# RWKV block inverse: 32x32 array tiles up to blocks of 32, key products inside the levels

## The reference

```python
def step(state, inp):
    r_t, w_t, k_t, v_t, a_t, b_t = inp
    sa = jnp.einsum('bhvk,bhk->bhv', state, a_t)
    state = state * w_t[:, :, None, :] + sa[..., None] * b_t[:, :, None, :] + v_t[..., None] * k_t[:, :, None, :]
    y = jnp.einsum('bhvk,bhk->bhv', state, r_t)
    return state, y
```

## Time and profile before

| | us |
|---|---|
| median of three runs | 1380.3 (lowest 1379.02, one at 3487.18) |
| the profiled execution | 1379.52 |
| its span | 1377.5 |
| TensorE busy in it | 1328.0 (96%) |
| VectorE busy | 869.5 (63%) |
| ScalarE busy | 354.0 (26%) |
| GpSimd busy | 119.6 (9%) |

### The profile page before, as it was taken

One profiled execution on the slowest core, in us unless ns is written; L12 is line 12 of the kernel. 1 busy time (PEld: TensorE's weight loads), 2 busy tenths in 40 slices (PEclk: granted clock), 3 DMA queues, 4 the chain that ended last, 5 costly groups with the idle time before them and its releaser, 6 DMA issues. The chain is left out here.

```text
span 1377.5 us, 24975 instructions
## 1 busy us (share of the span) xinstructions
PE 1328.0 (96%) x10772; PEld 1012.3 (73%) x10772; DVE 869.5 (63%) x1455; ACT 354.0 (26%) x755; POOL 119.6 (9%) x184
## 2 busy tenths in 40 slices
PE   7999999999999998899999999998999999999999
PEld 6868548689995444469998467847778765999943
DVE  4577612567778347538898567458444364798973
ACT  2311200312221014412332013703432331233300
POOL 5745000000000001010000000031000000000000
PEclk9999999999999999999999999999999999999999
DMA  8433224335444724045444543400011042454452
GB/s 303 173 129 134 104 91 153 130 138 184 175 145 171 249 73 166 0 153 184 175 145 171 206 160 123 184 1 3 4 33 34 27 160 91 154 183 147 161 183 92
DMA packets 16733, 182.30 MB, mean 132 GB/s; under 512 B 1648, under 2 KB 3952, under 8 KB 6000
## 3 DMA queue, kind: packets, MB, share of 16 engines
q1 hardware_dynamic: 14320, 175.12, 35.0%
q10 hardware_dynamic: 2304, 5.59, 1.1%
HBM read 179.65 MB, written 1.05 MB: 131 GB/s over the span
## 5 line engine op out<-in xcount | busy, mean ns | idle before, releaser
L1697 PE MATMUL banks<-xn,arena 128*128 128x128 f32 x1440 | 165.7, 275 | 0.0
L1697 PEld LDWEIGHTS banks<-xn,arena 128*128 128x128 f32 x1440 | 163.2, 192 | 0.0
L1714 PE MATMUL banks<-arena 128*128 128x512 f32 x264 | 122.0, 592 | 0.0
L1697 PE MATMUL banks<-hT,weight_ring 128*128 128x128 f32 x960 | 116.5, 275 | 0.0
L1697 PEld LDWEIGHTS banks<-hT,weight_ring 128*128 128x128 f32 x960 | 111.8, 192 | 0.0
L1423 PE MATMUL banks<-weight_ring,arena 128*128 128x512 f32 x224 | 98.7, 597 | 0.8 <-ACT arena L1313 0.8
L1714 PEld LDWEIGHTS banks<-arena 128*128 128x128 f32 x264 | 49.8, 190 | 60.7 <-issue 60.7
L1714 PE MATMUL banks<-weight_ring,arena 128*128 128x512 f32 x198 | 93.3, 592 | 0.0
L2642 DVE SCALAR_TENSOR_TENSOR arena<-arena,prm 128x255 f32<-128x255 f32 x200 | 87.4, 479 | 5.4 <-ACT arena L1068 3.6
L1423 PEld LDWEIGHTS banks<-weight_ring,arena 128*128 128x128 f32 x224 | 42.8, 193 | 51.9 <-issue 50.3
L3060 DVE COPY_PREDICATED weight_ring<-masks,banks 128x512 f32<-128x512 uint8 x48 | 35.1, 734 | 66.7 <-PE banks L2004 60.2
(11 more groups left out here) (443 smaller groups left out, 2204.7 us busy)
## 6 DMA issues: line engine op xcount, KB each, us to landing
weight_ring<-in_wall SPq DMA_DIRECT2D x81, 2048.0 KB, 8.2
weight_ring<-in_wall SPq DMA_DIRECT2D x2, 1024.0 KB, 7.2
x<-in_x_tok ACTq DMA_DIRECT2D x2, 512.0 KB, 4.6
arena<-in_mem_tok SPq DMA_DIRECT2D x1, 1024.0 KB, 17.4
arena<-in_wall SPq DMA_DIRECT2D x1, 1024.0 KB, 5.0
arena<-in_wide SPq DMA_DIRECT2D x2, 512.0 KB, 4.5
out_y<-x ACTq DMA_DIRECT2D x4, 256.0 KB, 2.0
arena<-in_masks ACTq DMA_DIRECT2D x1, 896.0 KB, 9.4
```

The lines of the kernel that those rows point to most:

```text
L1697: ins = mm(b_(n)[:, j * P:(j + 1) * P], lhsT=weights[:, kb, j * P:(j + 1) * P], rhs=features_[:, kb, :], start=opens and j == 0 and kb == ...
L1714: ins = mm(b_(n), lhsT=a, rhs=b, start=pair == 0, stop=pair == FB // 2 - 1)
```

## The change

Levels 1 to 4 and level 0 now work on blocks of 32: four 32x32 tiles on the diagonal of the array, one per 32 tokens, for eight heads per half. The inverse is kept both plain and turned (`T32`, index a), so a level needs no transposes: it has one product yl and two closing products tl. Masks repeat every 32 tokens. All four row tiles of a group write one PSUM bank (`narrow_`). The last level (32-blocks into 64) is made apart: `across_products` (group `yl..5`), `turned_diagonal` (`tf`), `turned_corners` (`to`), which ScalarE puts together in `inverse_out`. The inverse's buffer alternates between two steps, and GpSimd fills it earlier.

The order moves too: key products stand inside the levels, between yl and tl, and between the pieces of the last level; two or four `src` 1 products of a step come in the next step or at the step's end; the gates and `y_tokens(1)` come behind the last step's inverse. VectorE takes a level's copies ahead of the key product made inside that level. The order of the groups in `core_groups` is that of the TensorE code below; its removed lines are in the listing above.

```diff
-LEVELS = 6
+LEVELS = 5
...
+def core_groups(j):
+    last = j + 1 == len(STEPS)
+    later = (j, 1) if last else (j + 1, 0)
...
+    out += level_groups("yl", j, 1) + (key_products(j - 1, 1, 3) if j else key_products(0, 1, 0)) + level_groups("tl", j, 1)
...
+    out += level_groups("yl", j, 4) + key_products(*later, 0) + level_groups("tl", j, 4) + key_products(*later, 1)
...
-            b = 1 << v
-            off = (s // (2 * b) == l // (2 * b)) & (s // b != l // b) & later(s, l)
-            masks[:HD, d, 512 + HD * v:][:, :HD] = off[:HD, :HD]
-            masks[HD:, d, 512 + HD * v:][:, :HD] = off[HD:, HD:]
+            b, s_, l_ = 1 << v, s[:32], l[:, :32]
+            off = (s_ // (2 * b) == l_ // (2 * b)) & (s_ // b != l_ // b) & later(s_, l_)
+            masks[:, d, 512 + HD * v:][:, :HD] = np.tile(np.concatenate([off, off.T], axis=1), (4, 1))
...
+        def narrow_(n):
+            return bank[BANK_OF[n]].rearrange("p (a k c) -> p a k c", a=2, c=32)
+        def corners_(n):
+            return pair_(n)[:, :, 0:128].rearrange("p b (k c) -> p b k c", c=32)
...
-        T_rows = [half_of(lent[:, 2, 0, 0:1024], h) for h in HALVES]
-        Tc = [ap.rearrange("p (k b c) -> p b k c", k=4, b=2) for ap in T_rows]
-        Tt, Yb = [[quads(half_of(ap, h)) for h in HALVES] for ap in (lent[:, 2, 0, 1024:2048], lent[:, 2, 1, 0:1024])]
+        T32 = [lent[:, 2, 0, 1024 * i:1024 * i + 1024].rearrange("p (a k c) -> p a k c", a=2, c=32) for i in range(2)]
+        Yb = lent[:, 2, 1, 0:512].rearrange("p (k c) -> p k c", c=32)
...
+            def first_out(j, lv):
+                for h in HALVES:
+                    n = G[f"yl{j}{lv}{h}"]
+                    act.wait_ge(psum_full, n + 1)
+                    A(Yb[:, 8 * h:8 * h + 8, :], narrow_(n)[:, 0], ACT.Copy).then_inc(bank_sem(n), 1)
+            def inverse_out(j):
+                d = STEPS[j][0]
+                for h in HALVES:
+                    evict_pair(Tf[h], G[f"tf{j}{h}"])
+                for h in HALVES:
+                    n = G[f"to{j}{h}"]
+                    act.wait_ge(psum_full, n + 1)
+                    act.wait_ge(*when_read(G[f"tf{j}{h}"]))
+                    for r in (d, 2 + d):
+                        ins = A(Tf[h][QUARTER[r], :, :, QUARTER[1 - d]], corners_(n)[QUARTER[r]], ACT.Copy)
+                    ins.then_inc(bank_sem(n), 1)
...
+            def time_of(k, r):
+                at = (32 * r + (HD if k >= 4 else 0)) % P
+                return slice(at, at + 32)
+            def level_zero(j):
                 for h in HALVES:
...
+                    n, L = G[f"tl{j}0{h}"], heads(LA[STEPS[j][0]][h])
+                    free(n)
+                    for pp in range(2):
+                        pe.wait_ge(*when_read(G[f"ab{j}0{h}{pp}"]))
+                    for k in range(8):
+                        for a in range(2):
+                            for r in range(4):
+                                at = QUARTER[r]
+                                sides = (L[at, k, 0, time_of(k, r)], ident[at, at])
+                                ins = mm(narrow_(n)[at, a, k], lhsT=sides[a], rhs=sides[1 - a], start=True, stop=True,
+                                         tile_position=(32 * r, 32 * r))
+                    ins.then_inc(psum_full, 1)
+            def first_products(j, lv):
+                for h in HALVES:
+                    n, L, T_ = G[f"yl{j}{lv}{h}"], heads(LA[STEPS[j][0]][h]), T32[j % 2]
                     free(n)
                     pe.wait_ge(*when_read(G[f"tl{j}{lv - 1}{h}"]))
...
+                    for k in range(8):
+                        for r in range(4):
+                            at = QUARTER[r]
+                            ins = mm(narrow_(n)[at, 0, k], lhsT=L[at, k, 0, time_of(k, r)], rhs=T_[at, 0, 8 * h + k],
+                                     start=True, stop=True, tile_position=(32 * r, 32 * r))
+                    ins.then_inc(psum_full, 1)
+            def closing_products(j, lv):
                 for h in HALVES:
...
+                    n, T_ = G[f"tl{j}{lv}{h}"], T32[j % 2]
                     free(n)
                     pe.wait_ge(*when_read(G[f"yl{j}{lv}{h}"]))
...
+                    for k in range(8):
+                        for a in range(2):
+                            for r in range(4):
+                                at = QUARTER[r]
+                                sides = (T_[at, 1, 8 * h + k], Yb[at, 8 * h + k])
+                                ins = mm(narrow_(n)[at, a, k], lhsT=sides[a], rhs=sides[1 - a], start=True, stop=True,
+                                         tile_position=(32 * r, 32 * r))
+                    ins.then_inc(psum_full, 1)
+            def across_products(j):
+                d = STEPS[j][0]
+                for h in HALVES:
+                    n, L, T_ = G[f"yl{j}5{h}"], heads(LA[d][h]), T32[j % 2]
+                    free(n)
+                    pe.wait_ge(*when_read(G[f"tl{j}4{h}"]))
+                    for k in range(8):
+                        for side in range(2):
+                            first, second = 2 * side + d, 2 * side + 1 - d
+                            ins = mm(narrow_(n)[QUARTER[second], 0, k], lhsT=L[QUARTER[first], k, 0, time_of(k, second)],
+                                     rhs=T_[QUARTER[first], 0, 8 * h + k], start=True, stop=True,
+                                     tile_position=(32 * first, 32 * second))
+                    ins.then_inc(psum_full, 1)
+            def turned_diagonal(j):
+                for h in HALVES:
+                    n, T_ = G[f"tf{j}{h}"], T32[j % 2]
+                    free(n)
+                    pe.wait_ge(*when_read(G[f"tl{j}4{h}"]))
+                    for k in range(4):
+                        for swap in range(2):
+                            for r in range(4):
+                                to = r ^ (2 * swap)
+                                ins = mm(quads_(n)[QUARTER[to], swap, k], lhsT=T_[QUARTER[r], 0, 8 * h + 4 * swap + k],
+                                         rhs=ident[QUARTER[r], SIDE[r // 2]], start=True, stop=True,
+                                         tile_position=(32 * r, 32 * to))
+                    ins.then_inc(psum_full, 1)
+            def turned_corners(j):
+                d = STEPS[j][0]
+                for h in HALVES:
+                    n, T_ = G[f"to{j}{h}"], T32[j % 2]
+                    free(n)
+                    pe.wait_ge(*when_read(G[f"yl{j}5{h}"]))
+                    for k in range(4):
+                        for swap in range(2):
+                            for side in range(2):
+                                second, to = 2 * side + 1 - d, (2 * side + d) ^ (2 * swap)
+                                head = 8 * h + 4 * swap + k
+                                ins = mm(corners_(n)[QUARTER[to], swap, k], lhsT=Yb[QUARTER[second], head],
+                                         rhs=T_[QUARTER[second], 1, head], start=True, stop=True,
+                                         tile_position=(32 * second, 32 * to))
+                    ins.then_inc(psum_full, 1)
...
+            for i in range(4):
+                products(0, 0, i)
             for j in range(len(STEPS)):
...
+                later = (j + 1, 0) if j + 1 < len(STEPS) else (j, 1)
+                level_zero(j)
+                if j:
+                    products(j - 1, 1, 2)
+                if j == 2:
+                    tokens_of_keys(1, 0)
+                    tokens_of_keys(1, 1)
+                first_products(j, 1)
+                if j:
+                    products(j - 1, 1, 3)
+                else:
+                    products(0, 1, 0)
+                closing_products(j, 1)
+                for h in HALVES if j else ():
+                    x_start(j - 1, h)
+                first_products(j, 2)
+                for h in HALVES if j else ():
+                    block_solve(j - 1, h, "u1")
+                if j == 0:
+                    products(0, 1, 1)
+                closing_products(j, 2)
+                for h in HALVES if j else ():
+                    x_finish(j - 1, h)
+                if j == 0:
+                    pe.wait_ge(*when_read(G["bonus"]))
+                    transposes(G["tx_bonus"], [bonus_rows[:, tt * P:(tt + 1) * P] for tt in range(TT)])
+                first_products(j, 3)
+                for h in HALVES if j else ():
+                    block_solve(j - 1, h, "u2")
+                closing_products(j, 3)
+                for h in HALVES if j else ():
+                    y_out(j - 1, h)
+                first_products(j, 4)
+                products(*later, 0)
+                closing_products(j, 4)
+                products(*later, 1)
+                across_products(j)
+                products(*later, 2)
+                turned_diagonal(j)
+                products(*later, 3)
+                turned_corners(j)
+                if j == 0:
+                    tokens_of_keys(0, 0)
```

(69 more changed lines are left out.)

238 lines of the change are left out of this document (65 added, 173 removed).

## The result

The changed kernel takes **1521.45 us** (median of four runs, 1517.93 to 1523.48) against 1379.66 before: ratio 1.1031, interval 1.1001 to 1.1061, +142 us. The prediction said 1385, within 1362 to 1434.

The account below looks back on a forecast made before the run. TensorE, busy 1328.0 of 1377.5 us, was taken to bound the kernel. Work -12.7, waits that go -6.5 and waits that come +23.7 gave +4.5 us, so 1385 us on the median, range 1362 to 1434.

Parts of the forecast that it names:

- Price of a round: In the 32x32 inverse, one product on each tile side by side: 33 ns, bounds 27 and 60.
- rival A: In level 0, first and closing products, the round does not shrink from 60 ns: 1429 us, chance 13%.
- C: Rival: in the inverse, four row tiles writing one bank take turns, +177 us, 1562 us; chance 3%.
- Work, -12.7 us: TensorE's work on the inverse ahead of the turn of y: 88.7 us before, 76.0 after.
- Waits that go and come: TensorE's waits for VectorE's key product copies in the RWKV core: -6.5 us go, +23.7 us come.
- step 0: First step of the RWKV core: claimed to grow from 37.5 us to 42.
- Clock 1.00: In the RWKV core stage, TensorE's granted clock was claimed to stay at 1.00.
- rival E: TensorE's clock falls; at half, the inverse alone costs 76 us more, 1461 us; chance 2%.
- The arrival of instructions: Supply of TensorE's instructions in the RWKV core stage: hidden, 84 us if blocks come back to back.
- The sum of +4.5 us: Whole kernel: net of work saved, waits that go and waits that come, giving 1385 us on the median.
- rival B: Instructions arrive too slowly in the stage: 74 blocks at 3.1 us, 229 us for 191, 1423 us; chance 4%.
- The turn of y moves the end: Behind the inverse, y tile 1's turn at 1110.47 us feeds a long VectorE chain, so moving it moves the end.

Follow-up runs that it names:

- e12: Changed kernel, four heads' columns per stationary block in level 0, first and closing products (inverse not computed), VectorE taking key product first: 1383.85 us, 1.0041 of before.
- e7: Kernel before's 64x64 inverse in the change's order of work, but VectorE taking the key product ahead of the level's copies: 1378.78 us, 1.0005 of before.
- e1: Kernel before's 64x64 inverse in the change's order of work on all engines, VectorE copying the level first: 1402.14 us, 1.018 of before.
- e3: Changed kernel plus a filler product of 128x512 ahead of each of 72 groups of the inverse: 1524.73 us, 1.1066 of before.
- e4: Kernel before plus 1,024 one-column products (4,096 instructions) behind TensorE's last work: 1432.09 us, one run.
- e6: Changed kernel with VectorE taking the key product ahead of the level's two copies: 1507.23 us, 1.0935 of before.
- e9: Kernel before with the turn of y tile 1 moved ahead of the second gate: 1375.63 us, 0.9977 of before.
- e10: e7 with the turn of y tile 1 moved ahead of both gates: 1373.53 us, 0.9967 of before.

## Why the prediction was wrong, point by point

**Price of a round: right.** Before the supply runs short, level 0 of step 0 has 108 pairs in 0.91 us of TensorE's time:

```profile
928.50:929.50 1.00, 0.91 (x108) 0.94 (x110) 1.00 (x1) 0.00 (x0) 1.00 (x2) 1.00 0.00 0
```

8.4 ns a pair, 34 for a round of four against my 33. The first product's group is busy 0.74 (I had 0.72). That ends rival A. It ends C too: four row tiles write one bank here and do not take turns. The Trainium skill (TensorEngine Tiling (Array Packing), Restrictions and Gotchas) says that different row tiles cannot access one bank at the same time; taken as a price it would be four times this, and the measurement decides.

**Work, -12.7 us: not contradicted, and out of reach.** e12, which has the tiles and columns of the change and few instructions, is 8.2 us ahead of e7 at the gates, after 7.6 us of "issue" waits of its own and at a clock of 0.97. That fits the term in sign and size and does not measure it.

**Waits that go and come: right.** I had 23.7 + 1.2 = 24.9 us of waits for key products; e1 has 24.3. The net of the order was +17.2. In e1 the turn of y tile 1 comes 20.6 us later than before (1131.1 for 1110.5) and the median is 25.0 up; 2.5 us of it are TensorE's own work (busy 177.1 up to that turn for 174.6), at a clock of 0.95 for 1.00. The step 0 that I put at 42 us took 62.5 in the changed kernel (928.59 to 991.09), through blocks. In the changed kernel itself the waits for L3127 sum to 15.1 us; others of them lie under waits for blocks.

**Clock 1.00: wrong, as a consequence of the gaps.** e3 shows that the fall followed them, so rival E as a cause of its own falls. What the low clock costs where no block is missing (the key products are busy 48.9 us in the stage, for 33.9 in before) was not separated.

**The arrival of instructions: this is the step that failed.** The sum of +4.5 us has it at nothing, and rival B, which prices it at 1423 in all, had a chance of 4%. The runs show +135 us in its place, worked out below. B's count was near (18,494 TensorE instructions in the stage, for 18,900); three other things in it were wrong:

- *A block costs more.* I added the fetch (1.1 us) and the shortest transfer's latency (2.0) to 3.1; e4 has 3.71, 1.1 of fetch and 2.6 between.
- *It was taken as the larger of two totals*, 229 us of blocks or 191 of stage. Blocks and work overlap only where both are at hand: some 227 pairs ahead in e4, no more. The inverse is 4 x 2048 pairs, 64 blocks, 64 x 3.71 = 237 us in place of 76, while the key products and tails around it, with long products and few instructions, go on as before. That sum by stretch, an estimate, gives +161 us, less the blocks that come while a tail runs; measured, with the waits for VectorE out of the way, 122.2 + 12.7 = 135 ahead of the turn of y, 128.4 + 12.7 = 141 in the whole kernel (e6 against e7, and the work saved as predicted).
- *The demand was read over the stage.* 32 blocks of 1.1 us in 187 us looked like nothing. But a level's closing products are 256 pairs, 512 instructions, two blocks, in the 2.25 us that I had worked out: 1.1 us a block, which is the bare duration of a fetch with nothing between. Already with the cheapest reading of the earlier trace rows there was no slack at all in the densest group, and that asked for far more than 4%.

The sequencer's rate in before, 3 ns an instruction, was that of instructions that had arrived. It said nothing of how fast they do.

The Trainium skill (Runtime: NRT & Kernel Launch, Instruction fetch mechanics) says that instructions are fetched in blocks of 16 KB, 256 of them, the next while the current one runs. The trace agrees with the size: the gaps of e4 stand 128 pairs apart. The page also says that the fetch is "mostly hidden"; by that rule B would cost nothing, and for TensorE's small products e4 shows it wrong. It gives TensorE's buffer as 2048 instructions; in e4 the first gap comes after 454 of the small products' instructions.

**The turn of y moves the end: right.** It came 139.2 us late (1249.62 for 1110.47) and the span grew by 141.6; e9 and e10 moved it forward and the end followed, by as much as its wait behind the stage allowed. e12 shows where the rule ends: with the turn 0.6 us earlier than e7's the end came 4.4 us later, through a wait for a pair of banks and the clock.

## What to carry to other kernels

Count instructions by stretch before cutting a product into smaller tiles: a stretch whose TensorE work is under some 3.7 us per 256 instructions (14.5 ns each, 29 ns a pair) was bound by their arrival here, whatever the tiles could do, as far as blocks had not come ahead (some 227 pairs in e4). A smaller product is a gain only down to that line, and a level of the 64x64 inverse lay on it already: 136 pairs in a level of 3.9 us, 3.7 per 256 instructions. e7 has one gap of 2.0 us in a group of 64x64 products. When a producer on a slower engine has two things to read, give it first the one that is complete first: here that exchange alone was 23 us.

## What the runs showed of the hardware

- A block of 256 TensorE instructions takes 3.3 to 4.0 us to follow the last one where nothing else is in the way, at a clock of 0.50 (e4) and of 1.00 (3.83 in the changed kernel), and 2 to 3 us more beside full DMA queues (gaps of 3.5 to 4.7 us for 1.6 to 2.1 in e4).
- The gaps appear as "issue" in the list of waits, in the middle of a group of equal products. That they stand 128 pairs apart, with one transfer of the instruction queue to each, is what told this cause here.
- Gaps of 1.6 us after every 1.9 us of small products go with a granted clock of 0.50 (e4 from 1376 to 1428 us), and the work that follows gaps pays for it: the gates take 7.6 us longer in e12.
- Four 32x32 tiles on the diagonal, all writing one bank, take 34 ns for a product of 32 columns each, 111 for 128 (64 pairs in 1.95 us in e12: 16 rounds, the last 0.28).
